# Decode sample's read-out taken from the old state, its new state made in the mixing part, and moved loads, in a fused decoder layer on one core

## What is computed

```
z = x @ w_in
A: u = z_a * sigmoid(z_gate); c = silu(LN(causal depthwise conv of u, width 31, 512 channels))
B: token shift; r, k, v, decay w, rate a, gate g; per head (8 heads of 64 x 64):
   sa = S a ;  S' = S diag(w) + sa b^T + v k^T ;  y = S' r      # the delta rule, token by token
   o = (GroupNorm(y) + bonus) * g
x1 = LN(ALPHA * x + [c, o] @ w_out)
out = LN(ALPHA * x1 + shared expert(x1) + routed experts(x1))   # top 8 of 64 experts, 256 wide
```

## Time and profile before

| | us |
|---|---|
| median of 3 runs | 1228.48 (1227.61 to 1230.01) |
| the profiled execution's own time | 1227.23 |
| its span | 1225.4 |
| recurrence loop on PE, first step to the first `w_out` product | 261.90 to 360.51 |
| `w_out` products, layer norm, to the last x1 tile | 360.51 to 444.36 |
| shared expert and routing, to the block's end | 444.36 to 497.9 |
| experts | 497.9 to 1178 |

### The profile page before, as it was taken

One profiled execution on the slowest core, in us unless ns is written; L12 is line 12 of the kernel. 1 busy time (PEld: TensorE's weight loads), 2 busy tenths in 40 slices (PEclk: granted clock), 3 DMA queues, 4 the chain that ended last, 5 costly groups with the idle time before them and its releaser, 6 DMA issues. The chain is left out here.

```text
span 1225.4 us, 33477 instructions
## 1 busy us (share of the span) xinstructions
PE 1093.1 (89%) x14966; PEld 829.0 (68%) x14967; DVE 539.1 (44%) x1211; ACT 278.0 (23%) x579; POOL 190.9 (16%) x202
## 2 busy tenths in 40 slices
PE   6999997867799999899999999999999999989940
PEld 5878885656663575677777777777777667667720
DVE  0878968659764568352222222222222222222105
ACT  2155411221356120111111111111121111111102
POOL 2000100000000001022222222212222222212113
PEclk9999998966699999899999999999999999999975
DMA  6221231350234259799999999999999999999723
GB/s 201 69 54 50 56 87 37 53 180 5 83 102 128 104 181 394 243 345 342 340 344 348 339 337 329 325 318 331 321 330 324 328 335 326 338 325 337 255 41 140
DMA packets 87590, 279.59 MB, mean 228 GB/s; under 512 B 22363, under 2 KB 46948, under 8 KB 62605
## 3 DMA queue, kind: packets, MB, share of 16 engines
q1 hardware_dynamic: 72757, 242.20, 55.4%
q0 software_dynamic: 14336, 34.11, 11.5%
q10 hardware_dynamic: 352, 1.11, 0.3%
HBM read 258.80 MB, written 35.30 MB: 240 GB/s over the span
## 5 line engine op out<-in xcount | busy, mean ns | idle before, releaser
L2075 PE MATMUL pgu<-x_list_t,w_exp 128*64 128x96 f32 x8192 | 358.8, 248 | 16.1 <-DMA w_exp<-in_exp_up_dram 13.0
L2075 PEld LDWEIGHTS pgu<-x_list_t,w_exp 128*64 128x64 f32 x8192 | 343.6, 139 | 23.4 <-DMA w_exp<-in_exp_up_dram 16.8
L2102 PE MATMUL pyl<-w_exp,hid 128*96 128x512 f32 x512 | 231.8, 596 | 2.8 <-DMA w_exp<-in_exp_down_dram 1.8
L512 PE MATMUL pz<-w_exp 128*128 128x260 f32 (+1 forms) x736 | 171.1, 391 | 0.3 <-ACT w_exp L324 0.3
L2129 POOL DMA_INDIRECT scr_f<-y_list,row x64 | 92.4, 1444 | 503.7 <-DVE y_list L2120 172.6
L512 PEld LDWEIGHTS pz<-w_exp 128*128 128x128 f32 (+1 forms) x736 | 137.8, 190 | 28.1 <-issue 5.0
L2102 PEld LDWEIGHTS pyl<-w_exp,hid 128*96 128x96 f32 x512 | 80.6, 167 | 107.1 <-issue 105.9
L2090 DVE TENSOR_TENSOR sig<-sig,pgu 128x192 f32<-128x192 f32 x64 | 22.7, 354 | 289.8 <-ACT sig L2083 289.8
L2120 DVE TENSOR_SCALAR y_list<-pyl,weight 96x512 f32<-96x512 f32 x64 | 47.8, 747 | 204.8 <-PE pyl L2102 124.6
L2083 ACT ACTIVATE sig<-pgu 128x192 f32<-128x192 f32 x64 | 21.2, 331 | 388.6 <-PE pgu L2075 388.6
L161 DVE SCALAR_TENSOR_TENSOR w_exp<-arena,w_exp 128x512 f32<-128x512 f32 x120 | 90.0, 750 | 3.8
(11 more groups left out here) (341 smaller groups left out, 1014.8 us busy)
## 6 DMA issues: line engine op xcount, KB each, us to landing
w_exp<-in_exp_gate_dram SPq DMA_DIRECT2D x64, 1024.0 KB, 37.7
w_exp<-in_exp_up_dram SPq DMA_DIRECT2D x64, 1024.0 KB, 38.4
w_exp<-in_exp_down_dram SPq DMA_DIRECT2D x64, 1024.0 KB, 38.1
w_exp<-in_w_in_dram SPq DMA_DIRECT2D x22, 512.0 KB, 3.9
w_exp<-in_x_prompt_dram SPq DMA_DIRECT2D x8, 512.0 KB, 5.0
w_exp<-in_w_out_dram SPq DMA_DIRECT2D x2, 2048.0 KB, 14.2
scr_x<-arena SPq DMA_DIRECT2D x4, 512.0 KB
scr_f<-x_area SPq DMA_DIRECT2D x4, 512.0 KB, 3.6
```

The costliest lines, as they stand in the source:

```text
L512: last = nc.tensor.matmul(banks(pz[0:w, c % 2, :])[:, b, :], m.w_col[:, c % WB, k, 0:w], halves(m.x_t[:, k, :])[:, b, :], start=(k == 0), ...
L2075: last = nc.tensor.matmul(pgu[64 * half:64 * half + 64, s % 2, (2 * part + j) * CAP:(2 * part + j + 1) * CAP], w[job.slot][:, k, f0:P * ha ...
L2102: last = nc.tensor.matmul(pyl[0:CAP, c, :], hid[:, s % 2, j, :], m.expert_down[job.slot][:, j, c * 512:(c + 1) * 512], start=(j == 0), sto ...
```

## The change

The sample's read-out no longer needs the new state. Since S' = S diag(w) + sa b^T + v k^T, y = S (w r) + sa (b . r) + v (k . r). In the loop DVE now makes S a (steps 0 and 1, `sample_reads`), S (w r) (steps 2 and 3, `sample_kept_part`) and puts the rows together from two dot products (step 4, `sample_rows_out`). The new state itself (`sample_state`, two halves of five 128 x 1024 operations) is made after the loop: half 0 before `layer_norm(0)`, half 1 after `layer_norm(1)`. Fifteen more taps stand ahead of the first reads (19 in place of 4), two a step follow in steps 0 to 7, none later; the conv mean sums move from step 11 to 10 and the variance sums from 14 to 13. The x rows get space in slot 1 and wait for all moves; so expert 1's early loads go, experts 0 to 3 are loaded after x1, behind the store of the new state, and 2 and 3 wait for that store to land. POOL and ACT wait for the new state before they write over its inputs.

```
-    CONV = 11
+    TAPS_OVER = 8
+    CONV = 10
...
-                sp.wait_ge(sample_state_ready, 1)
-                sp.dma_start(m.new_wkv_s, st.rearrange("p v k -> p (v k)")).then_inc(sample_state_stored, 16)
...
-                for i in range(2):
-                    if i == 0:
-                        sp.wait_ge(sample_state_stored, 16)
-                    sp.dma_start(x_rows[:, i, :], m.x_prompt[i * P:(i + 1) * P, :]).then_inc(x_loaded[i], 16)
                 sp.wait_ge(w2_done, TM)
...
+                for i in range(2):
+                    if i == 0:
+                        sp.wait_ge(move_done, 2 * TM)
+                    sp.dma_start(x_rows[:, i, :], m.x_prompt[i * P:(i + 1) * P, :]).then_inc(x_loaded[i], 16)
...
-                load_gate_up(sp, m, 1)
...
-                sp.wait_ge(row_taken, use["gate", 3] + 1)
-                sp.wait_ge(conv_scaled, CT)
-                load_down(sp, m, 1)
...
-                for q in (0, 2, 3):
+                sp.wait_ge(sample_state_ready, 2)
+                sp.dma_start(m.new_wkv_s, st.rearrange("p v k -> p (v k)")).then_inc(sample_state_stored, 16)
+                for q in range(NB):
+                    if q == 2:
+                        sp.wait_ge(sample_state_stored, 16)
                     load_gate_up(sp, m, q)
                     load_down(sp, m, q)
...
+                def sample_state(part):
+
+                    vs = slice(part * SLICE, (part + 1) * SLICE)
                     values = lambda ap: ap[:, vs].unsqueeze(2).broadcast_to([P, SLICE, N])
                     s = st[:, vs, :]
...
+                    tt(s, s, keys(sv[:, 0, :]), ALU.mult)
+                    ch.link(tt(outer_late, values(sval), keys(sv[:, 3, :]), ALU.mult))
+                    ch.link(tt(s, s, outer_late, ALU.add))
+                    ch.link(tt(outer_late, values(s_a), keys(sv[:, 2, :]), ALU.mult))
+                    tt(s, s, outer_late, ALU.add).then_inc(sample_state_ready, 1)
+                    dve.wait_ge(sample_state_ready, part + 1)
...
-                taps.take(4)
+                taps.take(19)
                 add_reads(0)
...
-                    if n < 10:
-                        taps.take(min(3, CT * CW - m.taps_done))
-                        sample_slice(n // 5, n % 5)
+                    if n < TAPS_OVER:
+                        taps.take(min(2, CT * CW - m.taps_done))
+                    if n < 2:
+                        sample_reads(n)
+                    elif n < 4:
+                        sample_kept_part(n - 2)
+                    elif n == 4:
+                        sample_rows_out()
...
+                sample_state(0)
                 for i, (_, n) in enumerate(TOK_TILES):
                     layer_norm(i, n)
+                    if i == 1:
+                        sample_state(1)
...
-        m.x_again = place(m, m.UPPER, 2, D)
+        m.x_again = place(m, m.AT_ROWS + TM * DC, 2, D)
```

More of the change, by code:

```diff
@@ L982, in recur_and_mix @@
         s_y = view(m.arena, m.AT_BUSY + 3 * DC + 12 * H + 32, 32)
+        s_keys = view(m.arena, m.AT_BUSY + 3 * DC + 12 * H + 64, 2, N)
+        s_dots = view(m.arena, m.AT_BUSY + 3 * DC + 12 * H + 64 + 2 * N, 2)
+        outer_late = place(m, m.AT_ROWS + 2 * TM * DC, SLICE, N)
         sv, sval = m.sv, m.sval
@@ L1249, in _ @@
                 pool.wait_ge(mixed, NT)
+                pool.wait_ge(sample_state_ready, 2)
                 nc.gpsimd.memset(scores[:, TM, :], 0.0).then_inc(routing_consts, 1)
@@ L1732, in _ @@
                 act.wait_ge(routing_consts, 2)
+                act.wait_ge(sample_state_ready, 2)
                 act.wait_ge(logits_done, 1)
@@ L1802, in add_reads, with sample_reads @@
                     tt(r, r, p_read.rearrange("p b i d t -> p b i (d t)"), ALU.add).then_inc(read_taken, 1)
-                def sample_slice(part, op):
+                keys = lambda k: k.unsqueeze(1).broadcast_to([P, SLICE, N])
+                def sample_reads(part):
                     vs = slice(part * SLICE, (part + 1) * SLICE)
-                    keys = lambda s: sv[:, s, :].unsqueeze(1).broadcast_to([P, SLICE, N])
+                    if part == 0:
+                        dve.wait_ge(state_loaded, 16)
+                        dve.wait_ge(m.sample_loaded, 48)
+                    ch.link(tt(outer, st[:, vs, :], keys(sv[:, 1, :]), ALU.mult))
+                    ch.link(nc.vector.tensor_reduce(s_a[:, vs], outer, AX, ALU.add))
@@ new lines, in sample_kept_part, with sample_rows_out @@
+                def sample_kept_part(part):
+                    vs = slice(part * SLICE, (part + 1) * SLICE)
+                    if part == 0:
+                        ch.link(tt(s_keys[:, 0, :], sv[:, 0, :], sv[:, 4, :], ALU.mult))
+                    ch.link(tt(outer, st[:, vs, :], keys(s_keys[:, 0, :]), ALU.mult))
+                    ch.link(nc.vector.tensor_reduce(s_y[:, vs], outer, AX, ALU.add))
+                def sample_rows_out():
+                    ch.link(tt(s_keys, sv[:, 2:4, :], sv[:, 4, :].unsqueeze(1).broadcast_to([P, 2, N]), ALU.mult))
+                    ch.link(nc.vector.tensor_reduce(s_dots, s_keys, AX, ALU.add))
+                    ch.link(nc.vector.scalar_tensor_tensor(s_y, s_a, s_dots[:, 0:1], s_y, ALU.mult, ALU.add))
+                    nc.vector.scalar_tensor_tensor(s_y, sval, s_dots[:, 1:2], s_y, ALU.mult, ALU.add).then_inc(sample_y_ready, 1)
@@ L1808, in sample_slice @@
+                def sample_state(part):
+                    vs = slice(part * SLICE, (part + 1) * SLICE)
                     values = lambda ap: ap[:, vs].unsqueeze(2).broadcast_to([P, SLICE, N])
                     s = st[:, vs, :]
-                    if op == 0:
-                        if part == 0:
-                            dve.wait_ge(state_loaded, 16)
-                            dve.wait_ge(m.sample_loaded, 48)
-                        ch.link(tt(outer[:], s, keys(1), ALU.mult))
-                        ch.link(nc.vector.tensor_reduce(s_a[:, vs], outer[:], AX, ALU.add))
-                    elif op == 1:
-                        ch.link(tt(s, s, keys(0), ALU.mult))
-                        ch.link(tt(outer[:], values(sval[:]), keys(3), ALU.mult))
-                    elif op == 2:
-                        ch.link(tt(s, s, outer[:], ALU.add))
-                        ch.link(tt(outer[:], values(s_a[:]), keys(2), ALU.mult))
-                    elif op == 3:
-                        ch.link(tt(s, s, outer[:], ALU.add))
-                        last = tt(outer[:], s, keys(4), ALU.mult)
-                        if part == 1:
-                            last.then_inc(sample_state_ready, 1)
-                            dve.wait_ge(sample_state_ready, 1)
-                        else:
-                            ch.link(last)
-                    else:
-                        last = nc.vector.tensor_reduce(s_y[:, vs], outer[:], AX, ALU.add)
-                        if part == 1:
-                            last.then_inc(sample_y_ready, 1)
```

2 lines of the change are left out of this document (1 added, 1 removed).

## The result

The changed kernel takes 1245.66 us (median of 4 runs, 1244.81 to 1246.81) against 1229.24 us for the kernel before in the same comparison: a ratio of 1.0131, 95% interval 1.0109 to 1.0154, so 16 us slower. Timed again in another comparison (e5) the ratio was 1.0143 (1.0104 to 1.0181). The forecast was 1234.5 us and +6.0, range 1226.5 to 1240.0: slower, as forecast, but by nearly three times as much (16.4 us by the medians), and outside the range.

What follows compares the result with a forecast made beforehand. It took a PE and DVE chain to bound the loop, PE the stages after, and transfers the stretch behind x1; -11.9 + 5.7 + 2.2 + 10.0 = +6.0 us gave 1234.5 us, range 1226.5 to 1240.

Steps and rivals of the forecast that it cites:

- The loop: Steps up to the first `w_out` product: less DVE work gains 11.9 us, between 8.8 and 22.9.
- the replay: Loop: PE, DVE and ACT queues replayed with trace durations; pauses of 7.8 us stay, gain 8.8 us.
- the clock: Loop: blocks whose pause goes may run at 2.4 GHz, clearest in step 10; gain 3.1 us, between 0 and 14.1.
- the pauses before later steps: Loop: PE's pauses before steps after 4, with two taps or none as fill-in, should go.
- The taps in the gap: Ahead of the first `add_reads`: 15 more taps, 11.65 us, fit DVE's idle 11.58 us to within 0.1, at no cost.
- Ahead of the layer norm: `sample_state(0)` delays DVE: PE pauses 5.7 us before tile 2, plus 2.2 at the lower clock; `sample_state(1)` costs nothing.
- The queue: From x1 to the block's end: four more MB ahead of f's stores, 2.5 us each, cost 10.0 us.
- More waits than booked: Rival: loads delay token-row gathers and the experts, or tile 2's pause carries past x1; sum +9 to +12, chance 0.14.
- The faster ones: Rivals: clock up throughout the loop, 1223.5 us, chance 0.07; f's stores not waiting behind loads, about 1225, chance 0.07.
- Slower: Whole kernel: slower than before by over 0.2%, chance 0.70.

Runs made afterwards that it cites:

- e5: The changed kernel run again without edits, beside the kernel before: 1243.85 us, ratio 1.0143.
- e9: The kernel before run again without edits, for its own spread: 1228.07 us, ratio 1.0006.
- e4: Kernel before with only the three loads of expert 1 moved behind the stores of x1: 1237.81 us, ratio 1.0079.
- e1: Changed kernel with the new state's two halves placed behind the layer norms of tiles 1 and 2 on DVE: 1236.58 us, ratio 1.0066.
- e2: Changed kernel with the five stores of f issued by ACT on its own queue, not SP's: 1240.91 us, ratio 1.0086.
- e11: e8 with the conv's sums back in steps 10 and 13, as the changed kernel has them: 1224.29 us, ratio 0.9961.
- e3: Changed kernel with the conv's mean and variance sums back in steps 11 and 14: 1237.47 us, ratio 1.0055.
- e7: Changed kernel with the edits of e1 and e3 together: 1229.89 us, ratio 1.0028.
- e8: Changed kernel, sums in steps 11 and 14, new state in DVE's waits for ACT, 13 MB instead of 18 ahead of f's stores: 1216.65 us, ratio 0.9919.
- e12: e8 with the stores of f on ACT's queue: 1216.75 us, ratio 0.9912.
- e10: Kernel before with only the conv's sums moved to steps 10 and 13 from 11 and 14: 1238.25 us, ratio 1.0096.
- e6: Changed kernel with 16 conv taps and three of the sample's four read-outs left out of DVE's loop, outputs wrong: ratio 1.0129.

## Why the prediction was wrong

**The loop (the step that failed).** The forecast booked -11.9: 8.8 from the replay, which kept 7.8 us of pauses and took every other wait as it had been, and 3.1 from the clock. The replay's 8.8 was also the least that the loop could gain in the range. It gained 1.6 in the execution that was compared. Each loop is the sum of waits for DVE and ACT, issue waits and PE's busy time; means of the profiles, in us:

| | loops | waits for DVE, ACT | issue waits | busy | loop |
|---|---|---|---|---|---|
| before, e9, e4 | 3 | 16.5 | 2.7 | 78.3 | 97.8 |
| changed, e5, e1, e2, e11 | 5 | 10.5 | 6.1 | 75.7 | 92.6 |
| e3, e7, e8, e12 (sums in 11, 14) | 4 | 7.5 | 4.4 | 73.7 | 86.0 |

So the change is worth -5.2 on average: waits -6.0 where 8.8 had been forecast, busy time -2.6 where the clock's 3.1 had been, and issue waits +3.4 where nothing had been booked. In the compared execution they are -5.7, -0.9 and +5.0. The waits that the replay had too small are 1.45 before step 12 (0 forecast), 3.6 before step 4 (2.2) and 0.5 before step 2 (0); those before the variance sums and the last turn came as forecast or shorter (1.7 and 1.7, forecast 2.3 and 1.7).

**The shift of the sums.** It costs the changed loop 6.5 us, and the two groups don't overlap (85.1 to 86.9, 89.4 to 97.0): 3.0 are waits, 1.7 issue, 2.0 busy time. The replay had priced the pauses that it makes at their own length. Behind them the clock can fall, 5.43 in place of 3.77 us for the variance sums, but not in each execution: in e5 the same sums stood behind a longer wait, 2.17, and took 3.77. So the clock's term should have had a lower bound below 0: over the last six steps of the compared executions it was there (busy 36.7 against 35.1), and over the whole loop it was +0.9 (79.4 against 80.3), but below 0 against the two other loops of the kernel before (77.2 and 77.4). Four comparisons show the price of the shift itself in the total, by the ratios: 5 us from e8 to e11 and from e7 to e1, 9 from e3 to the changed kernel, 12 from before to e10.

**Instruction packets (a limit that was left out).** The forecast said that the pauses before later steps "should go". As waits for DVE they went, but the issue waits grew, because PE reached the end of the fetched instructions earlier. This had been in the trace: "issue" rows stood in the list of waits from which I took only DVE and ACT. Their growth is +5.0 in the compared executions and +3.4 in the means, since e9, with before's own code, has 4.6 of them. That the loop with the sums in 11 and 14 gains 11.8, as was booked for the loop with the sums in 10 and 13, is luck: -9.0 of waits, -4.6 of busy time and +1.7 of issue waits.

**The taps in the gap.** They cost nothing, as forecast: the changed kernel reaches step 1 after 5.23 us (269.37), before after 5.58. The gap was full to its end: `add_reads(0)` follows the last tap at 259.94 with no idle time, some 0.7 us after PE's reads were done, and nothing waited for it.

**Ahead of the layer norm.** Right in each number: the pause 5.42 (forecast 5.7, where its own operands give 5.6), the clock behind it 5.90 in place of 3.60 (2.3; forecast 2.2), together 7.7 of the 7.9 by which the stage grew. e1 and e7 show it by its absence. `sample_state(1)` cost nothing.

**The queue.** Right in mechanism, a little small: +10.0 forecast, +11.1 in the compared executions and 11.4 on average (792.2 over the five kernels that have 18 MB and the stores in SP's queue, without e6, whose outputs are others and which took 794.7; 780.8 over the three with 14). The term mis-sized is the MB: 2.85 in place of 2.5, most likely since gathers share the engines in that stretch. The limit of 358 GB/s that the prediction quotes from the Trainium skill ("DMA: Bandwidth & Descriptors", section "Specifications") would have given 2.93 per MB and 11.7, an estimate. But in the changed kernel the twelve loads behind the first still land 2.5 us apart (465.0 to 494.8), before the gathers come, so the agreement is not by that limit. What I had wrong is the reason: the store of f that DVE waits for is not the whole of what sets the end. e2 and e12 took it out of SP's queue; from x1 on e2 won 1.4 (and some 5 in all by its ratio), e12 nothing.

**The start.** The first step began at 264.14 and not at 261.90. Over all executions it is 260.9 to 263.6 in four with before's code on DVE, and 262.2 to 266.9 in ten with the changed one. The block itself begins late already (244.9 in place of 241.7 us), and nothing ahead of it was edited; of the edits only the fifteen taps run between it and the first step. In the compared execution the difference arises between 220 and 243 us, in a stretch granted a lower clock; in three others, and in e10, whose code on DVE is before's (263.6), it is there from the first 40 us on. It may be chance; no run settles it. Its mean, 264.2 against 261.9, is 2.3 us, and with it the means add up: 2.3 - 5.2 + 7.9 + 11.4 = 16.4, which is what the medians show.

**The rivals.** "More waits than booked" came nearest (+9 to +12). Its collision of loads and gathers was there, 2.7 us of which 1.6 came back, but the larger part was in the loop, where it had nothing. The faster ones had no part. "Slower" had 0.70 and came true; the range missed because every case kept the replay's 8.8 as the loop's floor, and none had the issue waits.

## What to carry to other kernels

When a step of work is moved earlier in a loop, list the waits that it makes for every engine that feeds it, and don't price them at their own length: 3.0 us of new waits cost 6.5 here on average, with what followed in issue waits and clock. Read the "issue" waits with the others: they are a second limit that takes back a part of what the first gave when it is lifted. Compare windows that hold the same work, and read an experiment in the steps that it changed. Work for which an engine has no deadline belongs in its waits, one operation at a time, and not in a block ahead of the step that frees a buffer; and of a transfer count the MB that are added to a stream that never stops, rather than the wait that ends last beside it.

## What was not expected of the hardware

- PE's instructions came in packets of 16 KB, 18 to 20 in a loop of some 2440 matmuls, never closer than 3.3 us, and PE went on 1.2 to 1.5 us after one had ended; with little else to wait for, it spent 11.8 of 92 us waiting for them.
- The same loop code took 89.4 to 97.0 us with nearly the same waits for other engines (10.1 to 10.8), at mean granted clocks of 0.75 to 0.83. One profile of each kernel could have shown this change's loop gaining 1.6 us or 9.2.
- A queue of its own did not give a store its own bandwidth: 8.8 us to landing for 0.5 MB beside the loads; one of before's last stores, issued at 492.77 with no load left in the queue, took 2.6.
